# Forming the diagonal of the tokens' scales ahead of VectorE's wait for constants and small parameters, in a two-layer decoder trunk

## What is computed

```
h    = rms_norm(x, norm1_g[l])            # x * r * g,  r = rsqrt(mean(x*x) + eps), one r per token
proj = h @ w_in[l]                        # 1024 x 3072: da_q, da_k, da_v, sb_q, sb_k, sb_v
q    = partial_rope(rms_norm(da_q, q_norm_g[l]), cos, sin)     # per head; k likewise
lam  = exp(sum(lambda_q1*lambda_k1)) - exp(sum(lambda_q2*lambda_k2)) + lambda_init
sb_q, sb_k, sb_v go into stick-breaking attention as they are, scaled by r
x    = x + concat(attentions) @ w_out[l]
x    = x + hierarchical_moe(rms_norm(x, norm2_g[l]), ...)
```

## Time and profile before

| what | value |
|---|---|
| median of 3 runs | 727.02 us (725.91 to 727.5) |
| the profiled execution, its own time | 726.92 us |
| its span, first to last instruction | 725.1 us |
| PE busy | 651.3 us, 90% |
| VectorE (DVE) busy | 257.7 us, 36% |
| ACT busy | 126.3 us, 17% |
| bytes moved by DMA | 239.09 MB, mean 330 GB/s |
| mean granted TensorE clock | 0.960 of full |

### The profile page before, as it was taken

One profiled execution on the slowest core, in us unless ns is written; L12 is line 12 of the kernel. 1 busy time (PEld: TensorE's weight loads), 2 busy tenths in 40 slices (PEclk: granted clock), 3 DMA queues, 4 the chain that ended last, 5 costly groups with the idle time before them and its releaser, 6 DMA issues.

```text
span 725.1 us, 12394 instructions
## 1 busy us (share of the span) xinstructions
PE 651.3 (90%) x4764; PEld 371.4 (51%) x4765; DVE 257.7 (36%) x557; ACT 126.3 (17%) x298; POOL 11.0 (2%) x22
## 2 busy tenths in 40 slices
PE   7899999999798995949999999999987989957796
PEld 4378555475545354425345865555644545524252
DVE  0444763254143132213224476531623332312033
ACT  3103342331000000000031035324200000000001
POOL 0002000000000000000030000000000000000000
PEclk9999999999899998879999999999999999979799
DMA  9789435766999999999999631296499999999995
GB/s 318 260 292 355 183 116 225 296 233 277 420 421 400 414 426 421 420 423 423 395 353 394 260 136 54 116 397 230 162 420 419 421 373 423 422 423 421 422 418 208
DMA packets 52599, 239.09 MB, mean 330 GB/s; under 512 B 8208, under 2 KB 8512, under 8 KB 28752
## 3 DMA queue, kind: packets, MB, share of 16 engines
q1 hardware_dynamic: 51984, 238.14, 82.2%
q0 software_dynamic: 576, 0.44, 0.5%
HBM read 237.52 MB, written 1.05 MB: 329 GB/s over the span
## 4 chain that ended last, share of the span: by engine, by line
PE 71%; DMA 17%; issue 4%; SPq 3%; DVE 3%; ACT 1%; DVEq 1%; ACTq 0%
DMA wbuf<-in_w_down 15%; PE bank L1235 12%; PE bank L1434 10%; PE bank L1404 10%; PE bank L1221 8%; PE bank L1379 8%; PE bank L1338 8%; PE bank L1443 6%; PE bank L1415 2%; DMA lamv<-in_lambda_k 2%; PE bank L1346 1%; PE bank L1294 1%; SPq L373 1%; PE bank L1268 1%; PE bank L1314 1%
## 5 line engine op out<-in xcount | busy, mean ns | idle before, releaser
L1235 PE MATMUL bank<-wbuf 128*128 128x512 f32 x256 | 113.1, 596 | 3.4 <-ACT wbuf L547 1.9
L1404 PE MATMUL bank<-wbuf,qkT 128*32 128x256 f32 x2048 | 113.8, 380 | 0.0
L1434 PE MATMUL bank<-wbuf,qkT 128*32 128x512 f32 x512 | 69.9, 692 | 44.3 <-DMA wbuf<-in_w_down 36.2
L1404 PEld LDWEIGHTS bank<-wbuf,qkT 128*32 128x32 f32 x2048 | 64.9, 110 | 52.1 <-issue 10.6
L1379 PE MATMUL bank<-qkT,x_sb 128*128 128x128 f32 x576 | 71.4, 284 | 11.1 <-issue 10.2
L1235 PEld LDWEIGHTS bank<-wbuf 128*128 128x128 f32 x256 | 47.7, 190 | 61.4 <-issue 57.1
L1379 PEld LDWEIGHTS bank<-qkT,x_sb 128*128 128x128 f32 x576 | 68.5, 198 | 14.3 <-issue 14.2
L1434 PEld LDWEIGHTS bank<-wbuf,qkT 128*32 128x32 f32 x512 | 17.9, 124 | 86.6 <-issue 77.3
L1443 PE MATMUL bank<-qkT 128*128 128x512 f32 x128 | 59.2, 605 | 0.0
L1221 PE MATMUL bank<-wbuf 128*128 128x256 f32 x256 | 56.5, 380 | 0.0
L1338 PE MATMUL bank<-wbuf 128*128 128x512 f32 x128 | 56.1, 594 | 0.0
(11 more groups left out here) (208 smaller groups left out, 517.6 us busy)
## 6 DMA issues: line engine op xcount, KB each, us to landing
wbuf<-in_w_gate SPq DMA_DIRECT2D x64, 1024.0 KB, 13.7
wbuf<-in_w_up SPq DMA_DIRECT2D x64, 1024.0 KB, 17.8
wbuf<-in_w_down SPq DMA_DIRECT2D x58, 1024.0 KB, 14.8
wbuf<-in_w_in SPq DMA_DIRECT2D x23, 1024.0 KB, 14.5
wbuf<-in_w_out SPq DMA_DIRECT2D x8, 1024.0 KB, 6.6
wbuf<-in_w_down SPq DMA_DIRECT2D x12, 512.0 KB, 9.4
x_sb<-in_x SPq DMA_DIRECT2D x2, 512.0 KB, 5.1
wbuf<-in_w_in SPq DMA_DIRECT2D x4, 256.0 KB, 5.0
```

The lines of the kernel that those rows point to most:

```text
L1235: last = MM(ps[PROJ_BANK[i][t]][:, :], hT[:, k, t * P:(t + 1) * P], block_rows(i, k), start=(k == 0), stop=(k == KC - 1))
L1404: last = MM(ps[bank][j * SLOTS:(j + 1) * SLOTS, 0:FF], hgT[:, k, j * SLOTS:(j + 1) * SLOTS], halves[:, at[j], k, :], start=(k == 0), stop= ...
L1434: last = MM(ps[DN_BANK[h]][j * SLOTS:(j + 1) * SLOTS, :], src[:, c, j * SLOTS:(j + 1) * SLOTS], at[j][:, c * D + h * HALF:c * D + (h + 1) ...
```

## The change

VectorE waits for `norm_r` and forms the diagonal first, and only then waits for `const_in` and `gains_in`. No instruction is added or removed.

```diff
                 for t in range(TT):
                     hT_half(2 * l, t, g1T)
+                dve.wait_ge(norm_r, 4 * l + TT)
+                for t in range(TT):
+                    V.tensor_scalar(rstd_diag[:, t * P:(t + 1) * P], ident, rstd[:, t:t + 1], None, ALU.mult)
+                gap().then_inc(diag_ready, 1)
+
                 if l == 0:
                     dve.wait_ge(const_in, 16)
                 dve.wait_ge(gains_in[l], N_GAINS)
-
-                dve.wait_ge(norm_r, 4 * l + TT)
-                for t in range(TT):
-                    V.tensor_scalar(rstd_diag[:, t * P:(t + 1) * P], ident, rstd[:, t:t + 1], None, ALU.mult)
-                gap().then_inc(diag_ready, 1)
                 prod = sq[:, 0:2 * HD].rearrange("p (n c) -> p n c", n=2)
```

More of the change, by code:

```diff
@@ L994, in _ @@
                     hT_half(2 * l, t, g1T)
-                if l == 0:
-                    dve.wait_ge(const_in, 16)
-                dve.wait_ge(gains_in[l], N_GAINS)
                 dve.wait_ge(norm_r, 4 * l + TT)
@@ L1002, in _ @@
                 gap().then_inc(diag_ready, 1)
+                if l == 0:
+                    dve.wait_ge(const_in, 16)
+                dve.wait_ge(gains_in[l], N_GAINS)
                 prod = sq[:, 0:2 * HD].rearrange("p (n c) -> p n c", n=2)
```

## The result

In the first measurement the changed kernel took 722.28 us (median of 6 runs, 720.98 to 723.51) beside 727.26 us for the kernel before (6 runs, 725.91 to 729.11): ratio 0.9935, interval 0.9914 to 0.9956, 5.0 us less. Measured again later, beside more runs of the kernel before, it took 722.6 against 725.62 us (ratio 0.9968, 0.9952 to 0.9985) and 722.64 against 725.66 us (0.9959, 0.9938 to 0.998). So the kernel is faster, by 3.0 us in the two larger measurements (1.1 to 3.5 and 1.5 to 4.5 us by their intervals), where 2.85 was forecast; the first measurement's 5.0 us lies above what the others show.

A forecast was written before the change was run, and what follows sets the result against it. It took TensorE's wait between layer 0's projections 0 and 1, behind the last lambda vector's load, as the bound: 3.70 − 0.85 = 2.85 us gained, 726.92 − 2.85 = 724.07, put at 724.2 us against the median; range 722.9 to 725.7 us.

The forecast's parts named there:

- The wait goes: Between projections 0 and 1 of layer 0, the diagonal comes some 10 us ahead of PE's need; 2.85 us gained.
- The constants, block 1 and the transposes' cover: Layer 0: constants land 3.6 us before PE comes, w_in's block 1 by 18.9 us; da_q's transposes keep 2.3 us.
- Layer 1 at nothing: The same reordering in layer 1 moves only waits satisfied long ago; gain set at 0.
- It reaches the end: The gain survives the full DMA stretch from 180 to 363 us, as its start moves earlier too; 2.85 us kept.
- The clock: TensorE's pause before projection 1 of layer 0 costs only its length, at 2.4 GHz; nothing added for slow matmuls.
- How the numbers follow: Whole kernel: gain 2.6 to 3.3 us at 0.84, single runs up to 1.1 us from their median, 0.8 us either side.
- within 0.25 us: From projection 1 to the first expert set, layer 0 takes 136.29 us and layer 1 136.04, so the stage moves whole.
- Rival A: Later weight loads in the full DMA stretch absorb the gain; time stays at 726.3 to 727.0 us; chance 0.08.
- B: More down-product groups in the expert stage run at the lower clock, 1.6 to 2.1 us each; slower; chance 0.05.
- Rival C of the prediction: Ahead of layer 0's row of scales, PE's wait for the constants replaces the diagonal's; 725.5 to 727.0 us; chance 0.03.

The follow-up runs named there:

- the long pause: Changed kernel with TensorE also waiting for block 2 of w_in ahead of layer 0's row of scales; 734.0 against 726.36 us, ratio 1.0108.
- diag_between: Changed kernel with the diagonal behind the wait for the constants but ahead of the small parameters' wait; 723.31 against 726.36 us, ratio 0.9956.
- layer0_only: Changed kernel with the move in layer 0 alone, layer 1 waiting as in the kernel before; 722.52 us, ratio 0.9964.
- before_again: The kernel before, unchanged, for a second trace; 726.14 against 725.62 us, ratio 1.0007.
- before_fifth: The kernel before, unchanged, for a fifth trace; 725.2 us in one run.
- before_third: The kernel before, unchanged, for a third trace; 725.74 us in one run.
- after_again: The changed kernel, unchanged, measured again with a second trace; 722.6 against 725.62 us, ratio 0.9968.
- after_third: The changed kernel, unchanged, measured once more beside the kernel before; 722.64 against 725.66 us, ratio 0.9959.

## Why the prediction was right or wrong

The range was wrong: 722.28 us lies 0.6 us under its lower end, and the first measurement's whole interval, 3.2 to 6.3 us, lies above the forecast 2.85. The two later medians of the changed kernel, 722.60 and 722.64 us, lie 0.3 us under that end too, though their gain of 3.0 us lies within the forecast 2.6 to 3.3. The removal of the wait was right, place by place; a term of the sum and the base that it was taken from were not.

- *The wait goes.* Diagonal at 12.09 us, row of scales 0.43 us, 2.84 us gained at the place, against 2.85 worked out from layer 1. The constants, block 1 and the transposes' cover held: the transposes of da_q start at 37.41 us, 0.6 us ahead of the 38.03 forecast, which is the earlier landing of the rest of block 0 in this execution (projection 0 goes on at 12.84 us instead of 13.47).
- *Layer 1 at nothing.* The move in layer 0 alone has the time of the whole move, to 0.1 us in the medians.
- *It reaches the end.* Shown both ways: by the changed kernel and by the long pause, whose 10.5 us were still 10.6 at projection 1 of layer 1.
- *The term that failed* is "The clock", in its sentence "So the pause costs only its length". That was read from one trace, and from a stretch of it that is the pause itself (24 to 27 us; the four microseconds behind it, 27 to 31 us, have 1.00 as well), and a slow clock got no chance of its own among the rivals. In five traces of the kernel before, the time from the last start of projection 0 to the end of projection 1 exceeds the 14.76 us without a pause by 2.84 (41.05 − 23.45 = 17.60), by 4.00 (41.64 − 22.88 = 18.76), by 2.31 (40.04 − 22.97 = 17.07), by 4.22 (41.90 − 22.92 = 18.98) and by 2.60 us (40.08 − 22.72 = 17.36): 3.2 us in the mean, where the larger measurements have 3.0. In the five traces of kernels without a pause (the changed one three times, diag_between, layer0_only) the clock was 1.00 at this place each time. The term should have stood in the sum as 0 to 1.7 us, the upper end being four matmuls of 0.43 us; in the mean of the five traces it is 0.7 us. That 2.85 lies so near is partly luck: the one trace that was read had the longest wait of the five (2.60 us against 2.07 to 2.36), so the length alone was sized 0.3 us too high. The Trainium skill's sentence on pauses in "TensorE: Matmul & The Clock Gate" (the section on why this matters for kernels), which the prediction set aside because one row disagreed, agrees with the long pause of 7.64 us; it is advice on longer gaps than the 2.07 and 2.29 us that the lower clock followed in two of the five traces, so for these the measurement decides.
- *The larger part of the miss is the base and its spread*, which "How the numbers follow" took from three runs. "Single runs lie up to 1.1 us from their median, a median of a few moves less" was too narrow: 80 runs of the kernel before, those of the first series and of the three later ones with more than one, lie from 722.88 to 729.81 us with a median of 726.02, and 30 runs of the changed kernel from 720.52 to 726.9 with a median of 722.64. Against these medians the forecast of 724.2 us is 1.6 us too high: 1.0 of it because its base of 727.02 lies above 726.02, and 0.5 because the gain is 3.4 by the medians (3.2 by the means) rather than 2.85. In the first measurement itself the base was near (727.26 us), and the gain was 2.1 us more than forecast; the five traces give 0.3 of these in the mean and 1.4 at most (4.22 − 2.85), so the rest is spread that no trace assigns.
- *A further place of spread* is the eight matmuls of L1358 ahead of the expert stage. PE's timelines of the kernel before in layer 1, in the first trace, in before_again and in before_fifth, have

```profile
508.21 3.68 PE L1358 MATMUL bank<-x_sb,cst 128*128 128x512 f32 x8
508.36 4.92 PE L1358 MATMUL bank<-x_sb,cst 128*128 128x512 f32 x8
506.50 5.17 PE L1358 MATMUL bank<-x_sb,cst 128*128 128x512 f32 x8
```

  and before_third has 5.22 us at 152.14 us in layer 0. There PE doesn't idle beforehand, it runs narrow matmuls (L1346); the granted clock is 0.53 in before_again from 509 to 511 us and 0.50 in before_third from 152 to 154 us, and the first gate product comes 1.4 to 1.7 us later. So the repeat "within 0.25 us" holds for the first trace and for none of the other four of the kernel before: in before_again layer 1 takes 519.96 − 382.26 = 137.70 us from projection 1 to the first expert set, where 136.04 was read. Three of the ten such places in the five traces of the kernel before were slow, and none of the ten in the five traces of kernels without a pause. If this hung on the pause, the gain would be 3.2 + (1.4 + 1.7 + 1.7) / 5 = 4.2 us in the mean, more than the interval of after_again allows (3.5) but within that of after_third (4.5). Against it, the two kernels whose pause was filled have a slow one each in layer 0. No run was made to test it, and it stays open.
- Where else the spread arises was seen (the landing of the first blocks, the length of the pause, the clock behind it, the clock within the expert sets) but not what sets it in a single execution. That stays open, and with it which level follows a pause of 2 us in a given execution, and why the first series shows 5.0 us rather than 3; five traces put the pause's own cost at 4.2 us at most.

Rival A is excluded by the long pause. B did not come: the chain of the kernel before has six groups of 32 down products of over 5 us, three in each layer, and so has that of the kernel after. In layer 0 it has

```profile
232.70 5.34 PE bank L1434 x32
...
287.83 5.75 PE bank L1434 x32
...
317.67 6.07 PE bank L1434 x32
```

where the first two were 5.34 and 5.87 and the third was 6.19. In layer 1 other groups are slow than before (5.08, 6.40 and 5.05 us, where 5.34, 5.92 and 6.02 were, the first of them in another set), so that the clock follows the pattern of waits within a set isn't shown. Rival C of the prediction did not come, as PE's row of scales shows no wait at all.

## What to carry to other kernels

A wait that an engine shares between two uses holds back the earlier one: look in the chain for a load that the work behind it doesn't read, and compare the place with the same place in a later layer, which prices the wait. Count behind a pause of TensorE also the matmuls that may run at the lower clock, and look at more than one execution before you say that they don't. Take the base and the spread for a range from more runs than three.

## What was not expected of the hardware

The same wait of 2.07 us left TensorE at 2.4 GHz in one execution and at 1.2 GHz for four matmuls in another, two of five in all; a pause of 7.64 us was followed by 0.50 and 16.09 us for projection 1. At L1358 the clock was 0.50 without any pause of TensorE ahead of it, in before_third from 152 to 154 us, where the first trace has 1.00 from 153 to 158 us.

Eighty further instructions of TensorE, far ahead of a loop, cost 110 us in that loop, with 78 packets of instruction loads instead of 23, and 256 further ones left the loads at 24. The Trainium skill ("Runtime: NRT & Kernel Launch", Instruction fetch mechanics) says that an engine's instructions are loaded in blocks of 256 and that a taken branch out of what is held makes the engine wait for a load; both counts agree with it. The change itself adds no instruction to TensorE, so nothing of this is in its result.
